# Two layers of a streaming encoder: silu of the gates at the projection's eviction, late queries of both heads in one instruction

## The reference, cut to what matters

```python
xn = _rms(x, norm_pre)
(aq, af, ai, ag, bq, bk, bv, bf, bg, cq, ck, cv, cg, ciq, cik, ciw, dq, dk, dv, dg) = split(xn @ w_in)   # 1024 x 4012
f_a = lb + (1 - lb) * sigmoid(af)                       # HGRN2: q = aq, k = 1 - f_a, v = ai, decay f_a
o_a, o_d = gla(aq, 1 - f_a, ai, log f_a), gla(rope(dq), rope(dk), dv, log gamma)
o_b = forgetting_attention(bq, bk, bv, log_sigmoid(bf + bias))
o_c = attention over the 256 keys with the largest sum_h relu(ciq_h . cik) * ciw_h      # the index
y = concat(head_rms(o_a) * silu(ag), o_b * silu(bg), o_c * silu(cg), head_rms(o_d) * silu(dg))
x = x + _rms(y @ w_out, norm_post)
```

## Time and profile before

| | us |
|---|---|
| median of 3 runs | 2507.97 |
| profiled execution, its own time | 2520.02 |
| its span, first to last instruction | 2518.3 |
| TensorE matmul busy | 2226.6 (88%) |
| VectorE busy | 1663.4 (66%) |
| ScalarE busy | 662.7 (26%) |
| GpSimd (POOL) busy | 349.0 (14%) |

### The profile page before, as it was taken

The page is one execution under the profiler, slowest core; times in us unless marked ns, Lnnn a source line. Parts: engine busy times, 40 slices in busy tenths (PEclk is TensorE's granted clock), DMA queues, the critical chain, the costliest instruction groups (busy, mean ns, idle before and its releaser), DMA issues. The chain is left out here.

```text
span 2518.3 us, 27658 instructions
## 1 busy us (share of the span) xinstructions
PE 2226.6 (88%) x9930; PEld 1328.1 (53%) x9930; DVE 1663.4 (66%) x3337; ACT 662.7 (26%) x1474; POOL 349.0 (14%) x436
## 2 busy tenths in 40 slices
PE   4999999978999877878869999999699998687887
PEld 3534544436777654545444445444377776454544
DVE  3356999995545587676333579999945456777772
ACT  3233100003333333322233420000033333323231
POOL 0000000000000243343200000000000012434341
PEclk9999999998999768887979999999899997788788
DMA  7111232121022211211041114221210222121101
GB/s 281 55 61 41 89 123 80 40 62 32 7 82 68 70 44 40 93 46 50 34 167 59 61 42 128 83 84 36 65 26 5 83 67 71 42 86 47 62 35 53
DMA packets 143304, 169.97 MB, mean 67 GB/s; under 512 B 69392, under 2 KB 97552, under 8 KB 142896
## 3 DMA queue, kind: packets, MB, share of 16 engines
q1 hardware_dynamic: 117696, 135.52, 16.7%
q10 hardware_dynamic: 25472, 32.66, 3.6%
HBM read 115.53 MB, written 62.50 MB: 71 GB/s over the span
## 5 line engine op out<-in xcount | busy, mean ns | idle before, releaser
L751 PE MATMUL ps<-wring,xnT_arena 128*128 128x512 f32 (+2 forms) x2304 | 883.0, 540 | 0.0
L751 PEld LDWEIGHTS ps<-wring,xnT_arena 128*128 128x128 f32 x2304 | 411.2, 190 | 444.5 <-issue 413.4
L1460 DVE TENSOR_SCALAR_CACHE_REDUCE arena<-arena,theta 32x1056 bf16<-32x1056 f32 x496 | 471.4, 986 | 8.8
L1049 PE MATMUL ps<-arena 128*128 128x128 f32 (+1 forms) x632 | 146.1, 364 | 146.6 <-DVE arena L1665 128.2
L1049 PEld LDWEIGHTS ps<-arena 128*128 128x128 f32 x632 | 109.6, 228 | 250.6 <-DVE arena L1665 200.6
L1151 ACT COPY arena<-ps 128x512 f32<-128x512 f32 (+1 forms) x128 | 70.0, 547 | 613.1 <-PE ps L751 613.1
L1552 DVE TENSOR_REDUCE small<-ps 128x1 f32<-128x192 f32 (+9 forms) x148 | 114.0, 771 | 153.3 <-PE ps L926 151.6
L1445 DVE SCALAR_TENSOR_TENSOR arena<-arena,iw 128x512 f32<-128x512 f32 (+6 forms) x224 | 135.7, 606 | 74.6 <-ACT arena L1200 67.8
L993 PE MATMUL ps<-wring,arena 128*128 128x512 f32 x320 | 178.2, 680 | 5.7 <-DVE arena L1607 5.7
L1297 ACT ACTIVATE arena<-ps,small 128x192 f32<-128x192 f32 (+9 forms) x148 | 111.0, 750 | 155.9 <-DVE small L1552 155.8
L993 PE MATMUL ps<-wring,xnT_arena 128*128 128x512 f32 x256 | 149.8, 713 | 0.0
(11 more groups left out here) (244 smaller groups left out, 2858.0 us busy)
## 6 DMA issues: line engine op xcount, KB each, us to landing
wring<-in_w_in SPq DMA_DIRECT2D x14, 2048.0 KB, 8.9
projected<-arena ACTq DMA_DIRECT2D x112, 256.0 KB, 2.0
arena<-residual SPq DMA_DIRECT2D x36, 512.0 KB, 5.1
arena<-projected SPq DMA_DIRECT2D x130, 128.0 KB, 3.5
arena<-projected SPq DMA_DIRECT2D x36, 384.0 KB, 3.7
residual<-arena SPq DMA_DIRECT2D x18, 512.0 KB, 2.7
wring<-in_w_out SPq DMA_DIRECT2D x8, 1024.0 KB, 6.0
out<-arena SPq DMA_DIRECT2D x16, 512.0 KB, 3.9
```

The costliest lines, as they stand in the source:

```text
L751: o = mm(bank(pbank(k), 0, b - a), xnT[:, c, t * P:(t + 1) * P], w, start=(c == 0), stop=(c == CH - 1))
L1049: o = mm(bank(level_bank(k), 2 * n_ * g, 2 * n_), keys[:, g * P:(g + 1) * P], queries[:, g].rearrange("p e n -> p (e n)"), start=True, sto ...
L1460: V.tensor_scalar(cmp_out[r, (i % 2) * WMAX:(i % 2) * WMAX + uw[u]], score[u][r], th_, 0.0, op, ALU.add, accum_out=into[r, i:i + 1]).then_ ...
```

## The change

`GROUPS` becomes lists of column ranges, ordered so that `projected` holds A's three blocks, D's three blocks and the four gates side by side; `kept(col)` gives a column's new place. The widths go from 296, 512, 512, 512, 132, 512, 512, 512, 512 to 296, 512, 388, 512, 512, 512, 512, 512, 256. A group's weights come in two DMAs. For the gates' columns (the second half of group 6, groups 7 and 8) the eviction applies Silu, with ScalarE's table set changed before and after. In the mix the gates' Exp, addition, reciprocals and product are gone, and `gated` multiplies by `LG`; the load of a tile three later waits for `x_y` and has 3 DMAs. The sigmoid is Exp, Ln, Exp on ScalarE. `QFA`, `QFD` and `QL` are laid out head first, and one VectorE instruction per level multiplies `QFA` (with its zeros) by `E`.

```diff
-GROUPS = [(CIQ, DQ)] + [(c, min(c + 512, CIQ)) for c in range(BQ, CIQ, 512)] + [(c, c + 512) for c in (*range(0, BQ, 512), *range(DQ, N_IN, 512))]
+GROUPS = [[(CIQ, DQ)], [(BQ, BV)], [(BV, BG), (CK, CG)], [(CQ, CK), (AQ, AF)], [(AF, AG)], [(DQ, DV)], [(DV, DG), (AG, BQ)], [(BG, CQ), (CG, CIQ)], [(DG, N_IN)]]
-G_ATT = 1 + -(-(CIQ - BQ) // 512)
+G_ATT = 4
+SILU = {6: 256, 7: 0, 8: 0}
...
 def mix_loads(t):
     if t >= 3:
         sp.wait_ge(x_su, x_su_at[t - 3])
-        sp.wait_ge(x_g, x_g_at[t - 3])
+        sp.wait_ge(x_y, x_y_at[t - 3])
...
-        for i, col in enumerate((AG, BG, CG, DG)):
-            sp.dma_start(LG[t % 3][:, i, :], prj_d[r, col:col + 256])...
+        for tile_, col in ((LA[t % 3], K_A), (LD[t % 3], K_D), (LG[t % 3], K_G)):
+            n = tile_.shape[1]
+            sp.dma_start(tile_, prj_d[r, col:col + 256 * n].rearrange("p (a n) -> p a n", a=n))...
...
 # evacuate, tiles 1 to 8 (tile 0 the same on its two halves)
-nc.scalar.copy(stage[s][:, 0:n], bank(pbank(k), 0, n)).then_inc(p_ev, 1)
+plain = SILU.get(g, n)
+if plain:
+    o = nc.scalar.copy(stage[s][:, 0:plain], bank(pbank(k), 0, plain))
+    if plain < n:
+        o.then_inc(act_own, one_more(own))
+        act.wait_ge(act_own, own[0])
+if plain < n:
+    o = A(stage[s][:, plain:n], bank(pbank(k), plain, n - plain), ACT.Silu)
+o.then_inc(p_ev, 1)
...
             A(lf_t1, lf_t1, ACT.Ln, bias=C("one")).then_inc(lf_ln, 1)      # after group G_ATT + 1
+            act.preload_act_table_set("silu_and_others")
...
+act.preload_act_table_set("natural_log_exp_and_others")                    # after the last eviction
...
 def start_forget(t):
     A(sig[t % 2], LA[t % 3][:, 1, :], ACT.Exp, scale=-1.0)
-    A(sig[t % 2], sig[t % 2], ACT.Identity, bias=C("one")).then_inc(x_sig, 1)
+    A(sig[t % 2], sig[t % 2], ACT.Ln, bias=C("one"))
+    A(sig[t % 2], sig[t % 2], ACT.Exp, scale=-1.0).then_inc(x_sg, 1)
-def start_gates(t): ...      -def sigmoid(t): ...      -def gates(t, i): ...      -def silu(t): ...
...
 # the levels on VectorE
-for e in range(2):
-    r = slice(HD * e, HD * e + HD)
-    V.tensor_tensor(QL[k[1] % 2][r, :, e, :].rearrange("p g (b i) -> p g b i", i=size // 2),
-                    cut_(QKA[:, 0])[r, :, :, size // 2:], cut_(E[k[1] % 2])[r, :, :, size // 2:], ALU.mult).then_inc(x_ql, 1)
+if i == 0:
+    dve.wait_ge(x_qf, 2 * x_qf_at[t])
+blocks = lambda x: x.rearrange("p (m s) -> p m s", s=size)[:, :, size // 2:]
+V.tensor_tensor(QL[k[1] % 2].rearrange("p e g (b i) -> p e (g b) i", i=size // 2),
+                QFA.rearrange("p e g (b s) -> p e (g b) s", s=size)[:, :, :, size // 2:],
+                blocks(E[k[1] % 2])[:, None].broadcast_to([P, 2, 2 * P // size, size // 2]), ALU.mult).then_inc(x_ql, 1)
...
 # the levels on TensorE
-       queries[:, g].rearrange("p e n -> p (e n)"), start=True, stop=True)
+       queries[:, :, g, :], start=True, stop=True)
...
 def gated(t):
-    pool.wait_ge(x_g, x_g_at[t])
-    e = eg[t % 2]
+    e = LG[t % 3]
```

More of the change, by code:

```diff
@@ L39, with kept @@
 CQ, CK, CV, CG, CIQ, CIK, CIW, DQ, DK, DV, DG = 2052, 2308, 2372, 2436, 2692, 2948, 2980, 2988, 3244, 3500, 3756
-GROUPS = [(CIQ, DQ)] + [(c, min(c + 512, CIQ)) for c in range(BQ, CIQ, 512)] + [(c, c + 512) for c in (*range(0, BQ, 512), *range(DQ, N_IN, 512))]
+GROUPS = [[(CIQ, DQ)], [(BQ, BV)], [(BV, BG), (CK, CG)], [(CQ, CK), (AQ, AF)], [(AF, AG)], [(DQ, DV)], [(DV, DG), (AG, BQ)], [(BG, CQ), (CG, CIQ)], [(DG, N_IN)]]
 NG = len(GROUPS)
 NIX = DQ - CIQ
-G_ATT = 1 + -(-(CIQ - BQ) // 512)
+G_ATT = 4
+GW = [sum(b - a for a, b in ranges) for ranges in GROUPS]
+GP = [sum(GW[:g]) for g in range(NG)]
+SILU = {6: 256, 7: 0, 8: 0}
+def kept(col):
+    for g, ranges in enumerate(GROUPS):
+        at = GP[g]
+        for a, b in ranges:
+            if a <= col < b:
+                return at + col - a
+            at += b - a
+    raise ValueError(col)
+K_BQ, K_BK, K_BV, K_BF, K_CQ, K_CK, K_CV, K_A, K_D, K_G = (kept(c) for c in (BQ, BK, BV, BF, CQ, CK, CV, AQ, DQ, AG))
 def width(t):
@@ L279, in encoder @@
         QFA, QFD = cx([2, 2, P]), cx([2, 2, P])
-        QL = [split[:, i, :].rearrange("p (g e n) -> p g e n", g=2, e=2) for i in range(2)]
+        QL = [split[:, i, :].rearrange("p (e g n) -> p e g n", g=2, e=2) for i in range(2)]
         KL = [split[:, 2 + i, :] for i in range(2)]
@@ L570, in w_group @@
                     def w_group(g):
[L571 to L573 removed]
+                        dst = wring[:, CH * 512 * (g % 2):CH * 512 * (g % 2) + CH * GW[g]].rearrange("p (c n) -> p c n", c=CH)
+                        at = 0
+                        for a, b in GROUPS[g]:
+                            parts = 2 // len(GROUPS[g])
+                            for i in range(parts):
+                                rows = slice(CH // parts * i, CH // parts * (i + 1))
+                                sp.dma_start(dst[:, rows, at:at + b - a],
+                                             w_in[at_layer, :, a:b].rearrange("o (c p) n -> p (o c) n", p=P)[:, rows]).then_inc(ld_w[ld_w_slot[g]], 16)
+                            at += b - a
                     def x_tile(t):
@@ L750, in project @@
                             else:
-                                o = mm(bank(pbank(k), 0, b - a), xnT[:, c, t * P:(t + 1) * P], w, start=(c == 0), stop=(c == CH - 1))
+                                o = mm(bank(pbank(k), 0, wide), xnT[:, c, t * P:(t + 1) * P], w, start=(c == 0), stop=(c == CH - 1))
                             if c == CH // 2 - 1 and (k, 0) in IX_SLOTS:
@@ L1346, in _ @@
                             r = slice(HD * e, HD * e + HD)
-                            nc.scalar.copy(QFA[r, :, e, :], QKA[r, 0].rearrange("p (g n) -> p g n", g=2)).then_inc(x_qf, 1)
+                            nc.scalar.copy(QFA[r, e, :, :], QKA[r, 0].rearrange("p (g n) -> p g n", g=2)).then_inc(x_qf, 1)
                         exps = [k for k in EXPS if k[0] == t]
@@ L1569, in _ @@
                     dve.wait_ge(attend_end["P"], 1)
-                    def gates(t, i):
-                        if i == 0:
-                            dve.wait_ge(x_eg, x_eg_at[t])
-                        o = V.reciprocal(eg[t % 2][:, i], eg[t % 2][:, i])
-                        if i < 3:
-                            o.then_inc(dve_own, one_more(own))
-                        else:
-                            dve.wait_ge(dve_own, own[0])
-                            o.then_inc(x_er, 1)
                     def residual(t):
@@ L1671, in _ @@
                                 take(levels[-1])
-                            if i == 2 and t + 1 < NT:
-                                sigmoid(t + 1)
                             if i == 6 and t >= 1:
                                 turned_y(t - 1)
-                        if t == 0:
-                            for i in range(4):
-                                gates(0, i)
-                        if t + 1 < NT:
-                            gates(t + 1, 0)
                         if t >= 2:
                             residual(t - 2)
-                        if t + 1 < NT:
-                            gates(t + 1, 1)
                         dve.wait_ge(x_su, x_su_at[t])
```

90 lines of the change are left out of this document (33 added, 57 removed).

## The result

The changed kernel takes 2407.1 us, median of 4 runs (2401.9 to 2409.2), where the kernel before has 2507.7 on the same chip: a ratio of 0.959, 95% interval 0.957 to 0.961. That is 100.6 us less; forecast were 108, and 2400. The profiled execution of the changed kernel took 2407.3 us, its span is 2405.3 and its mean granted clock 0.939 (before 0.918). Between the two profiled spans lie 113 us, since the one of before stood above its median.

The account below looks back on a forecast made before the run. TensorE's columns bound it until the index search; in the mix levels VectorE, with TensorE waiting. -27 - 50 - 27.5 - 3.5 = -108 takes the median from 2508.0 to 2400 us; own range 2385 to 2415, 8 in 10 within 2360 to 2450.

Parts of the forecast that it names:

- Columns regrouped: In the projection, 124 columns leave the stretch ahead of the index search; it begins 13.3 us earlier per layer, -27 in all.
- Silu at the eviction: In the projection, ScalarE's copies become Silu, hidden behind its waits for TensorE: 0.
- the reading by which the table loads are on the path: Two ScalarE table switches a layer, 2.66 us each, would make the sum 11 us smaller if on the path.
- Late queries merged: In the mix levels, 122 pairs of VectorE instructions become 122 single ones: 56 us saved, about 6 given back, -50.
- per pair 1.136 - 0.677: Pair's mean time less that of the similar instruction L1624: 0.46 us saved a pair, times 122 is 56 us.
- The plain price: Late-query saving when POOL does not collide, 0.59 against 0.43 us: 0.16 a pair, 20 us, the lower bound.
- The first rival, POOL's joined run: POOL's run without its gap meets levels one to five; merged instructions wait like pairs, the 50 lost: 2450, chance 0.18.
- one lock met and not two: Each merged late-query instruction is shut out by POOL once instead of twice, putting the gain above the plain 0.16.
- Reciprocal off: The sigmoid's VectorE reciprocal, 1.72 us, goes; 16 of 18 stand inside the mix levels: -27.5.
- TensorE's clock, a rival with 36: Shorter waits keep TensorE at 2.4 GHz; 3 us go in 12 middle tiles, another 36: 2364, chance 0.20.
- Gates off: The mix gates' work goes; covered in middle tiles, only two reciprocals after tile 0 count: -3.5 for both layers.
- Loads, the two-piece queries, the copy `x_qf`: Fewer, later DMAs, L1049's queries read in two pieces, and the merged instruction's wait for ScalarE's copy: 0 each.

## Why the prediction came out right, and where its steps failed

*Columns regrouped, -27: right.* 13.45 and 13.5 us by the traces, and 24 of 27 by the time of the kernel with the widths back. The cover was there: 7 us of TensorE's idle time were to be left, and 8 are.

*Silu at the eviction, 0: right.* ScalarE still waited 153.7 us for TensorE ahead of 32 evictions with Silu, 256 columns of which take 0.38 us. The table load behind the last of them is one row of the groups (two layers); above it, from ScalarE's timeline of the first layer, the load ahead of the first of them with the instructions on either side:

```profile
399.78 0.33 ACT L1249 ACTIVATE arena<-arena,cf 128x36 f32<-128x36 f32 x1
400.12 1.28 ACT L1250 ACT_TABLE_LOAD   x1
401.82 0.37 ACT L1166 COPY arena<-ps 64x256 f32<-64x256 f32 x1 [0.41 <-PE ps L764]
...
L1260 ACT ACT_TABLE_LOAD x2 | 2.6, 1283 | 0.8 <-ACT arena L1181 0.8
```

The Trainium skill ("ScalarE: Activation LUTs", What ACT_TABLE_LOAD costs) gives the load itself as about 1283 ns, which is this row's figure, and a whole switch as the 2.66 us that the prediction used. The measured switch is shorter: from the end of the instruction before the load to the start of the next one pass 1.7 us (400.11 to 401.82), 0.41 of them put down to TensorE. The load behind the last Silu ran beside TensorE's idle time ahead of the fox keys (1739.41, the keys at 1749.46), and the reading by which the table loads are on the path, 11 us, did not come true.

*Late queries merged, -50: mis-sized in the sum.* The step that failed is "per pair 1.136 - 0.677": it took means that hold collisions, and assumed that a collision goes when its instruction goes, whatever else is changed. The plain price, 0.59 - 0.41 = 0.18 a pair, stood beside it as the lower bound (as 0.16), and in VectorE's busy time that is about what came behind the sigmoid: 18.1 us in the changed kernel (264.6 - 246.5), 19.5 without collisions (161.0 - 141.5). In the levels' time it depends on what else is in place. Ahead of the sigmoid and at a held clock the merge takes 3.1 us off a middle tile (24.9 to 21.8), 0.44 a pair and so nearly the forecast's 0.46; behind the sigmoid 2.1 (22.94 to 20.84), 0.30 a pair; without collisions 0.78, 0.11 a pair. So the price fitted the kernel in which it was read, and not the sum with the next term. In time the merge is worth some 11 to 22 us on top of the other edits. The first rival, POOL's joined run, named the right engine and half of the mechanism: the merged instruction did not wait as long as its pair, 0.75 us against 1.14, but the decays and the late keys behind it took over what it no longer met.
The Trainium skill ("SBUF — State Buffer", Who interferes with whom) has the two engines shut each other out for whole instructions. The traces agree: 1.48 us beside POOL, 0.41 alone. The prediction's reading, one lock met and not two, was wrong in this: the lock is met by whichever two-input product comes next.

*Reciprocal off, -27.5: mis-sized in the sum.* 5 to 13 us on top of the other edits; 2.0 us a middle tile alone with the clock held, more than its 1.72, and 0.95 with the merge in place. The 1.72 us had a second use that was not priced: while VectorE ran the reciprocal, which has one input, POOL could not start `forget`, and what it would have met ran free (8.0 us less in the three products with the reciprocal back). In tile 0 that second use was the larger.

*TensorE's clock, a rival with 36: came in beside the forecast.* The prediction had it as a case that excludes the forecast; it was a term. Over the middle tiles the levels of before stood 30 us above 24.9, those of the changed kernel were in three tiles low again (22.4 instead of 20.84), 5 us: 25 net. So the levels' 80.2 are 25 of the clock and, by subtraction, 55 of VectorE, where 77.5 were forecast of VectorE alone: the 22 that were missing and the 25 that were not in the sum are of one size by luck.
Of the 22, some 6 lie in the twelve middle tiles (4.06 at a held clock, where 2.87 + 1.72 was forecast). The rest lies where the forecast spread the same prices over tiles that gave less: 7.5 in tile 0, whose levels did not get shorter at all (16.98 and 16.50 us before, 16.96 and 16.59 after), 6 in tile 1 and 2.6 in tile 8.
The prediction's reading that the falls go with TensorE's waits for the late queries holds in part: filling the waits removed them, but the waits alone do not bring them, as tile 2 of the second layer shows.

*Gates off, -3.5: right in kind*, 5.6 by the traces, all of it ahead of tile 1. *Loads, the two-piece queries, the copy `x_qf`, 0:* no run takes them alone. In the changed kernel's trace VectorE did not wait ahead of the late queries (idle 0.0 in their row above), and a level's four matmuls take 0.71 us in both kernels (2199.54 after; 2202.55 before, at the same clock).

What is open: behind the levels the rest of a middle tile takes about 14.9, 16.4 or 17.9 us over the kernels, at a mean granted clock of 0.89, 0.79 or 0.71, so the difference is how long the clock is low in TensorE's outputs; why one tile gets the one and the next another, and why tile 2 of the second layer kept its clock in the kernel before, no run here settles.

## What to carry to other kernels

Do not price an instruction that another engine can shut out by its mean alone: the waiting in the mean belongs in large part to the other engine's work, and moves to the instruction's neighbours when it goes. Take the free duration as the lower bound, and add up two such terms only after trying each without the other. To be rid of the waiting, move that work to where the first engine has nothing of the kind (here 88 us by two moved calls and a wait, against 11 to 22 for the merge). And where two edits both shorten one engine's waits, test each alone: a clock that holds is had once, and whichever edit comes first seems to earn it.

## What the runs showed of the hardware beyond expectation

Twelve spare matmuls a tile made the kernel 24 us faster: filling TensorE's waits kept the granted clock at 1.00 where it had been 0.60, and eight transposes went from 1.91 to 1.04 us. The Trainium skill ("TensorE: Matmul & The Clock Gate", What's actually happening) says that activity releases the clock; this is that rule at work on idle slots. What tips it is not settled here: in the kernel before, one middle tile kept 1.00 with waits no shorter than those of the other eleven, which fell.

VectorE's waiting beside POOL changed little with the number of its instructions (112 and 104 us in two kernels with 488 VectorE products in the levels, 105 in one with 366, all with POOL's run in the levels), and the overlap cost POOL too: `forget`'s first product took 0.91 us beside VectorE and 0.73 alone.
